# Crowded experts' branch and next norm's sums inside the combining block, a store in four parts, attention output in three passes

## The reference, cut to what matters

```python
def rmsnorm_2(x, g):
    xf = x.astype(jnp.float32)
    y = xf * lax.rsqrt(jnp.mean(xf * xf, axis=-1, keepdims=True) + EPS)
    return (y * g.astype(jnp.float32)).astype(x.dtype)

# first block, attention layer
x = x + nsa_attention(rmsnorm(x, norm_mix[i]), w_in_b[j], w_out_b[j], cos, sin, kv)   # ends in  o @ w_out

# second block, each layer l
xl = xl + m_l[:, 2] * y_l                       # mixer (even: layer 0, odd: layer 1)
hl = rmsnorm_2(xl, norm_ffn_g[l]) * (1.0 + m_l[:, 4]) + m_l[:, 3]
xl = xl + m_l[:, 5] * moe(hl, router_w, router_b, moe_w_gate[l], moe_w_up[l], moe_w_down[l])
...                                             # the same for the context, layer 0 only
return rmsnorm_2(xl, final_norm_g)
```

## Time and profile before

| what | value |
|---|---|
| median of 3 runs | 2408.97 us (2406.07 to 2411.21) |
| the profiled execution | 2410.38 us, span 2408.6 us |
| mean granted TensorE clock | 0.944 of 2.4 GHz |
| TensorE busy | 2147.7 us (89%) |
| VectorE busy | 1673.3 us (69%) |
| ScalarE busy | 1365.1 us (57%) |
| GpSimd busy | 277.2 us (12%) |
| DMA | 454.95 MB, mean 189 GB/s |

### The profile page before, as it was taken

How to read it: one execution, slowest core, us unless ns; L and a number is a source line. 1 busy time by engine, 2 the same in 40 slices (tenths; PEclk the granted TensorE clock), 3 DMA queues, 4 the chain that set the end, 5 groups by cost and what they waited for, 6 DMA issues and landing times. The chain is left out here.

```text
span 2408.6 us, 36095 instructions
## 1 busy us (share of the span) xinstructions
PE 2147.7 (89%) x12262; PEld 1755.4 (73%) x12262; DVE 1673.3 (69%) x2798; ACT 1365.1 (57%) x2135; POOL 277.2 (12%) x357
## 2 busy tenths in 40 slices
PE   4999899989998999978888799996689997899993
PEld 4899876679996666666666587785478886677782
DVE  5884635358646488987773599996547864799993
ACT  2664414347545245675542588885467863688882
POOL 0000000000000056556200011011000000101000
PEclk8999999999998999989999799998799998899996
DMA  6455331355543666610012499998121221799991
GB/s 224 160 184 174 123 138 52 131 193 193 175 146 103 250 230 234 238 55 1 19 61 70 177 380 389 389 390 318 69 97 62 72 96 62 290 393 396 393 358 70
DMA packets 127253, 454.95 MB, mean 189 GB/s; under 512 B 13824, under 2 KB 17792, under 8 KB 126976
## 3 DMA queue, kind: packets, MB, share of 16 engines
q1 hardware_dynamic: 116160, 413.14, 47.4%
q0 software_dynamic: 10944, 39.85, 4.4%
HBM read 431.97 MB, written 20.97 MB: 188 GB/s over the span
## 5 line engine op out<-in xcount | busy, mean ns | idle before, releaser
L2720 DVE TENSOR_TENSOR moe_w_lo<-ring,moe_w_hi 128x1024 fp32r<-128x1024 f32 x384 | 462.5, 1221 | 61.3 <-ACT moe_w_hi L2658 56.3
L2658 ACT CAST moe_w_hi<-ring 128x1024 fp32r<-128x1024 f32 x384 | 399.0, 1049 | 130.2 <-PE ps L236 120.1
L373 DVE TENSOR_TENSOR ffn_w_lo<-ring,ffn_w_hi 128x1024 fp32r<-128x1024 f32 x132 | 161.0, 1222 | 101.2 <-ACT ffn_w_hi L325 101.0
L234 PE MATMUL ps<-moe_w_hi,moe_own 128*128 128x512 f32 x512 | 214.2, 418 | 12.0 <-DVE moe_own L2727 11.1
L235 PE MATMUL ps<-moe_w_lo,moe_own 128*128 128x512 f32 x512 | 205.2, 401 | 0.0
L236 PE MATMUL ps<-moe_w_hi,moe_own 128*128 128x512 f32 x512 | 205.0, 400 | 0.0
L325 ACT CAST ffn_w_hi<-ring 128x1024 fp32r<-128x1024 f32 x132 | 137.4, 1044 | 107.4 <-PE ps L236 107.4
L234 PE MATMUL ps<-ffn_h_hi,ffn_w_hi 128*128 128x256 f32 x608 | 173.3, 285 | 11.2 <-DVE ffn_w_lo L373 11.2
L235 PE MATMUL ps<-ffn_h_lo,ffn_w_hi 128*128 128x256 f32 x608 | 172.0, 283 | 0.0
L236 PE MATMUL ps<-ffn_h_hi,ffn_w_lo 128*128 128x256 f32 x608 | 172.0, 283 | 0.0
L234 PE MATMUL ps<-ffn_hid,ffn_w_hi 128*128 128x256 f32 x448 | 131.0, 292 | 12.8 <-DVE ffn_w_lo L373 9.0
(11 more groups left out here) (547 smaller groups left out, 5584.8 us busy)
## 6 DMA issues: line engine op xcount, KB each, us to landing
ring<-in_weights SPq DMA_DIRECT2D x766, 512.0 KB, 5.4
expert_rows<-moe_y POOLq DMA_DIRECT2D x32, 512.0 KB, 7.1
token_rows<-moe_token_rows SPq DMA_DIRECT2D x6, 512.0 KB, 3.2
sq<-in_cmp_w SPq DMA_DIRECT2D x1, 2048.0 KB, 8.3
both<-in_x SPq DMA_DIRECT2D x1, 1024.0 KB, 5.8
both<-in_context SPq DMA_DIRECT2D x1, 1024.0 KB, 8.0
out<-both SPq DMA_DIRECT2D x1, 1024.0 KB, 4.8
cols<-in_cols SPq DMA_DIRECT2D x1, 720.5 KB, 9.1
```

Source lines behind the costliest of these rows:

```text
L234: pe.matmul(out, w_hi, x_hi, start=start, stop=False)
L373: dve.tensor_tensor(w_lo[:, u % WB], k.ring[:, (first + u) % RING], w_hi[:, u % WB], ALU.subtract).then_inc(w_split, 1)
L2658: act.copy(w_hi[:, j % WB].rearrange("p h f -> p (h f)"), k.slot(act, first + GU + j, e).rearrange("p a f -> p (a f)")).then_inc(w_rounded, 1)
L2720: dve.tensor_tensor(w_lo[:, j % WB].rearrange("p h f -> p (h f)"), k.ring[:, (first + GU + j) % RING].rearrange("p a f -> p (a f)"), w_hi[ ...
```

## The change

Four things, besides names:

- `linear_residual` does products 1 to 7 in three passes. ScalarE casts each weight slot and the input (in four parts of two tiles), VectorE subtracts; two buffers for the parts. Product 0 stays plain fp32. ScalarE's silu of the condition now stands behind the first weight cast and the four input casts. The modulation product of step m is issued ahead of product m (m from 1), the last one ahead of product 6; the turn of the modulation stands ahead of product 7, its keeping ahead of the last add.
- The count's load and the crowded experts' branch go ahead of the combining: the load stands before the block, the branch opens it on its four engines, and the combining follows in the same block.
- The combining block also computes the next normalization's squares (into the token rows' space, used up by then), sums, root and reciprocal, per segment of 256 tokens. An add waits only for its own bank's transposes. In the first layer VectorE's order is mix 0, 1, 2, three adds, mix 3, the other adds; TensorE sums half of the first segment's squares before the last tile's transposes. The root's table is loaded by a small root ahead of the squares.
- The odd mixer starts with the weight splits and goes on to the scaling; the last block scales `x` (`final_scale_store`) and issues a store after each two tiles.

The diff, cut:

```diff
 def linear_residual(...)
+            def _(act):
+                def round_w(m):
+                    if m > WB:
+                        act.wait_ge(product, m - WB + 1)
+                    act.copy(w_hi[:, m % WB], k.slot(act, first + m * PER)).then_inc(w_rounded, 1)
+                round_w(1)
+                for t in range(0, TILES, 2):
+                    act.copy(in_hi[:, t:t + 2, :], inp[:, t:t + 2, :]).then_inc(in_rounded, 1)
+                act.activation(padded[:, :, 0:2], cond, ACT.Silu).then_inc(mod_ready, 1)
...
+                pe.wait_ge(mod_ready, 2)
+                mod_part(0)
+                for m in range(1, KD):
+                    if m < KD - 1:
+                        mod_part(m)
+                    if m == KD - 2:
+                        mod_part(KD - 1)
+                    if m == KD - 1:
+                        pe.wait_ge(mod_taken, 1)
+                        mod_turn(k, pe, rows, TURN_BANK).then_inc(mod_turned, 1)
...
+                        mm = product_of_parts(pe, k.ps[:, m % BANKS, 0:n], (w_hi[:, m % WB, t, :], w_lo[:, m % WB, t, :]),
+                                              (in_hi[:, t, :], in_lo[:, t, :]), t == 0, t == TILES - 1)

 def final_scale_store(k, x, gain, out):
+            for t in range(KD):
+                dve.scalar_tensor_tensor(x[:, t, :], x[:, t, :], gain[:, t:t + 1], k.rstd[:, 0:T], ALU.mult, ALU.mult).then_inc(normed, 1)
...
+            for t in range(0, KD, PER):
+                sp.wait_ge(normed, t + PER)
+                sp.dma_start(out[:, t:t + PER, :], x[:, t:t + PER, :]).then_inc(stored, 16)

 def moe(...)
-            moe_combine(k, x, segs, gate, name, tt_n, pick, share, rows, y_hbm)
-        fullest = nc.values_load(most[0:1, 0:1], min_val=0, max_val=n, ...)
-        moe_late(k, x, segs, gate, name + "_late", n, tt_n, first, late, fullest)
+            fullest = nc.values_load(most[0:1, 0:1], min_val=0, max_val=n, ...)
+            moe_combine(k, x, segs, gate, name, n, tt_n, first, pick, share, rows, y_hbm, late, fullest)

 def moe_combine(...)        # each engine's branch `If(fullest > P)` stands ahead of these
+                for tt in range(PER):
+                    turn(tt)
+                if len(segs) > 1:
+                    turn(PER)
+                    sums(0, range(KD // 2))
+                    turn(PER + 1)
+                    sums(0, range(KD // 2, KD))
+                sums(len(segs) - 1, range(KD))
...
+                act.activation(k.root[:, 0:1], k.eps[:, 0:1], ACT.Sqrt)
+                for j, s in enumerate(segs):
+                    for m in range(KD):
+                        act.wait_ge(x_made, j * KD + m + 1)
+                        act.activation(squares(j)[:, m, :], x[:, m, s * T:(s + 1) * T], ACT.Square).then_inc(squared, 1)
...
+                for tt in range(PER):
+                    mix(tt)
+                if len(segs) > 1:
+                    mix(PER)
+                    add(0, range(3))
+                    mix(PER + 1)
+                    add(0, range(3, KD))
+                add(len(segs) - 1, range(KD))
+                for j in range(len(segs)):
+                    dve.wait_ge(rooted, j + 1)
+                    dve.reciprocal(k.rstd[:, j * T:(j + 1) * T], k.root[:, j * T:(j + 1) * T])

 def odd_mixer(...)
-                    norm_tensor(k, pe, norm, T2)
-                    mod_norm_root(k, act, norm, x, first_splits)
+                    first_splits()
```

More of the change, by code:

```diff
@@ L1175, in linear_residual @@
     cond, bias, mods, weights, gains = modulated
[L1176 to L1203, removed]
@@ L1463, in mod_norm_high, with mod_norm_split @@
                            bias=shift[:, t, j:j + 1]).then_inc(rounded, 1)
[L1466 to L1469, removed]
+def mod_norm_split(k, dve, x, gain, shift, made, rounded, h_hi, h_lo, h_split, by_column=False):
     for t in range(KD + 1):
@@ L2810, in _, with moe_combine @@
                 pick_rows()
-def moe_combine(k, x, segs, gate, name, tt_n, pick, share, rows, y_hbm):
+def moe_combine(k, x, segs, gate, name, n, tt_n, first, pick, share, rows, y_hbm, late, fullest):
     nc = k.nc
     other = k.sq[:, :, :].rearrange("p a b -> p (a b)").rearrange("p (t d) -> p t d", d=D)
[L2817 to L2857, removed]
@@ L2871, in moe_late, with _ @@
         act_g = sb("act_g", [P, 2, n])
[L2872 to L2875, removed]
+        with stage_semaphores(nc, f"{name}_combine", "read", "spread", "diag_made", "product", "gated", "hidden", "down", "added",
+                              "scaled", "mixed", "turned", "x_made", "squared", "summed", "rooted", *[f"got{t}" for t in range(tt_n)]
+                              ) as sems, nc.Block(name=f"{name}_combine", no_gpsimd_drain=True) as block:
+            read, spread, diag_made, product, gated, hidden, down, added = sems[:8]
+            (scaled, mixed, turned, x_made, squared, summed, rooted), got = sems[8:15], sems[15:]
+            @block.gpsimd
+            def _(pool):
+                for tt in range(tt_n):
+                    for c, to in enumerate((rows, other)):
+                        pool.indirect_dma_start(out=to[:, tt, :], out_offset=None, in_=y_hbm,
+                                                in_offset=bass.IndirectOffsetOnAxis(ap=pick[:, c, tt:tt + 1], axis=0)
+                                                ).then_inc(got[tt], 16)
             @block.sync
@@ L2918, in _, with turn, sums @@
                             mm.then_inc(down, 1)
+                def turn(tt):
+                    j = tt // PER
+                    pe.wait_ge(mixed, tt + 1)
+                    for m in range(KD):
+                        at = m % BY_BANK * T + tt % PER * P
+                        mm = pe.transpose(k.ps[:, j * 4 + m // BY_BANK, at:at + P], rows[:, tt, m * P:(m + 1) * P], k.ident[:, :])
+                        if tt % PER == PER - 1 and m % BY_BANK == BY_BANK - 1:
+                            mm.then_inc(turned, 1)
+                def sums(j, ms):
+                    for m in ms:
+                        pe.wait_ge(squared, j * KD + max(m + 1, BY_BANK))
+                        mm = pe.matmul(k.ps[:, j, 0:T], k.ones[:, :], squares(j)[:, m, :], start=(m == 0), stop=(m == KD - 1))
+                    if m == KD - 1:
+                        mm.then_inc(summed, 1)
+                for tt in range(PER):
[6 more added lines that the diff above has]
+                sums(len(segs) - 1, range(KD))
             @block.scalar
@@ L3604, in build_program @@
         second_block(k, both, col, tri, hmask, reset, slot_number, tok_number, modulated, (masks[:, 2 * P:6 * P + T2], ins["masks"][:, 2 * P:6 * P + T2]))
[L3605 to L3611 removed]
+        final_scale_store(k, x, col("final_g"), out)
 def lay_out(a):
```

133 lines of the change are left out of this document (97 added, 36 removed).

## The result

The changed kernel took 2385.67 us (median of four runs, 2377.85 to 2387.04) against 2409.83 for the kernel before (2406.07 to 2411.21, four runs): a ratio of 0.9898 with a 95% interval of 0.988 to 0.9915. The forecast was 2384.0, in a range of 2377 to 2393. The profiled execution had 2387.04 us, with a span of 2385.3.

A forecast was written before the change was run, and what follows sets the result against it. TensorE is busy 89% of the span; the change touches the attention output and two seams where it stands still. Gains 6.0 + 7.6 + 11.6 = 25.2 us turn 2410.4 into 2385.2, expected median 2384.0, range 2377 to 2393.

The forecast's parts named there:

- Attention output: Stage with products 1 to 7 in three rounded passes: next stage starts at 490.1 instead of 496.1, 6.0 us gained.
- the late silu: Attention output: silu behind one weight cast and four input casts delays the first modulation product, adding 1.0 us of wait.
- the hidden splits: Attention output: ScalarE's casts and VectorE's subtractions need 2.3 of each 3.84 us step, so they are hidden.
- the loads from the ring: Attention output: twelve blocks in the ring at the start keep weight loads hidden, some 2.5 us to spare.
- Rival (2): Attention output follows its loads and gains nothing, giving 2390 us; chance 0.06.
- First seam: After the first experts' combining: the next stage's first TensorE product at 1714.5 instead of 1722.16, 7.6 us gained.
- The mix order gains nothing: First seam: second segment's adds end at 1700.9, hardly earlier than before, because sums stand ahead of the last transposes.
- the 4.6 of bare splits: First seam: weight splits, formerly beside the sums, now stand bare ahead of the scalings, 4.56 us from cast to last subtraction.
- End: After the last experts' combining: earlier adds, sums and four stores end the span at 2397.0 instead of 2408.6, 11.6 us gained.
- Branch hidden: Both seams: TensorE's late jump over the untaken branch is covered by the gather; uncovered it would cost 3.4 us each.
- Rivals (1): Sums keep the low clock in both seams, 4.5 and 1.8 us less gained, giving 2390 us; chance 0.13.
- (3): TensorE is granted 1.2 GHz in the attention output, making the kernel slower at 2412 us; chance 0.02.

The follow-up runs named there:

- slots_by_split: Changed kernel with SyncE reloading an attention-output weight slot once VectorE has made its low part, not after TensorE's product: 2381.6 us, ratio 0.9895 to before.
- before_no_branch: Kernel before without the crowded experts' branch and the count's load: 2397.6 us, ratio 0.9954 to before.
- turns_first: Changed kernel with TensorE turning all four tiles in the first seam before it sums any squares: 2381.19 us, ratio 0.9878 to before.
- one_store: Changed kernel with one store of 1 MB after the last scaling instead of four: 2382.65 us, ratio 0.9889 to before.
- attn_only: Kernel before with the new attention output alone: 2401.18 us, ratio 0.996 to before.
- jump_moved: Kernel before with 113 more TensorE instructions, long-fulfilled waits, ahead of the second experts' transposes: 2407.58 us, ratio 0.9992 to before.

## Why the prediction was right

The forecast of each place was right in its mechanism, but each place was off in size, by -2.3, +1.7 and +1.4 us. That these cancel to 0.8 is luck, and so is part of the end: five other kernels with the same end, whose sums ran longer (5.6 to 5.9 us), gained 11.2 to 11.5 there and not 13.0. The stated 2384.0 is also 0.2 above what the sum gives, 2408.97 less 25.2.

- **Attention output, 6.0 forecast, 3.7 measured.** The pass of 0.118 (0.120 measured), the late silu, the hidden splits and the loads from the ring held. What failed is the step "the add 0.47: 489.4 ... The next stage starts at 490.1": it took the barrier's 0.72 from the old kernel, where SyncE's last issues lay beside the modulation's tail. With the tail moved ahead of product 7, three issues follow the last product and hold the barrier 1.24 us longer; slots_by_split took 1.2 of it away. The rest, 1.1 us over the products, is the turn between fp32 and rounded passes, 0.2 a step. Rival (2) falls, since TensorE's only wait in the stage was the 1.0 us for the silu.
- **First seam, 7.6 forecast, 9.3 measured.** The branch's share is 4.9 (before_no_branch), the rest 4.4. GpSimd's load of the count cost nothing to be seen: copy to first gather is 5.7 us in both kernels, where 0.5 had been put. The sums ended 34.0 after the copy and not 35.8, as the clock rose about 2 us sooner than assumed: the last eight transposes already ran at the full level, in 1.04 us instead of 1.8. "The mix order gains nothing" held (turns_first), and so did the 4.6 of bare splits; that taking them away gives nothing in the end was not foreseen.
- **End, 11.6 forecast, 13.0 measured.** Of it 5.2 are what before_no_branch gained and 2.6 the four stores; the other 5.2 are the early adds and squares, with the clock in them: the same sums took 4.29 us in the profiled execution, 4.25 to 4.37 in three other kernels and 5.6 to 5.9 in six. Against the forecast the sums were 0.8 shorter (5.05 had been put), and a store lands in 2.2, not 2.9. The estimate by the Trainium skill (DMA: Bandwidth & Descriptors, Anatomy of one DMA), 2.6 for a store of this size, was nearer than the row of a load, though that section gives its numbers for DMAs issued by GpSimd and these were SyncE's. The fixed part wasn't paid four times on the path, as one_store shows.
- **Branch hidden**: held to 0.3 us, though the profile after doesn't show the jump itself, which had been named as a sign. That most of its cost hangs on the place of the code wasn't known; both old seams happened to have the late jump.
- **Rivals (1) and (3)** fall too: the sums at the end took 4.29 us, and not the 6.8 of the low clock throughout, and in the attention output the granted clock was 1.00 (464 to 493).
- The unedited stretches took 2.8 us more in the profiled execution, which no step had.

## What to carry to other kernels

A block that opens while a transfer is in flight is the place for untaken branches, table loads and other waits that no data needs: a branch, its count's load and its block cost about 5 us in a gap of their own, and the branch cost 0.3 at most beside the gather. When work is moved ahead of a stage's end, look at who is then last at the barrier, the queue that issues reloads too. And a product that starts earlier while the clock rises no earlier gives back a part of what it gained: here 1.0 of 2.6 us at once.

## What the runs showed of the hardware

At an untaken branch over some 400 TensorE instructions (an estimate from the kernel's text) TensorE came 3.4 to 3.8 us after ScalarE at four places, in the kernel before and in the first seams of attn_only and jump_moved, and 0.3 to 0.5 after it at two places where 113 more instructions stood ahead. Not every place with more instructions ahead is a cheap one: attn_only's first seam has them too and was 3.4 late.

Stretches without any edit fall into levels: the start to the attention output took 453.0, 455 to 456 or 459 us, and the stretch to the first experts' end 1164 to 1165 or 1168 to 1172. The clock goes with it, as the same stretch of the changed kernel and of one_store shows:

```profile
...
257.00:459.00 202.00, 186.93 (x1112) 142.41 (x1111) 105.11 (x297) 80.64 (x234) 4.13 (x5) 0.95 0.27 92
...
```

```profile
...
257.00:453.00 196.00, 180.75 (x1104) 137.26 (x1102) 104.49 (x294) 78.78 (x231) 3.88 (x5) 0.97 0.28 95
...
```

With 0.95 it takes 202 us, with 0.97 it takes 196, and the medians of the kernel before lie about as far apart, 2403.24 to 2410.11 in five sets. What picks the level stays open. In the same way the sums at the end took 4.3 or 5.6 to 5.9 us. Effects of 1 or 2 us in this kernel can be read off the timeline, where TensorE's clock in the stretch is looked at too, and not off the medians of four runs.
